# The last product of the first output tile, moved from VectorE to GpSimd in an encoder layer with a mixture of experts

## The chip, the cores and the metric

The kernel runs on one core of a Trainium2 chip. The metric is the device time of one execution in microseconds (us); three executions of the kernel before are given by their median. A profiled execution has a span of its own, from its first to its last instruction.

## What is computed

One layer of a bidirectional encoder on 512 tokens of width 1024, all in float32: attention in three dilated windows and a short gated convolution, a mixture of 32 experts of which each token takes 4, and a final RMS norm. What the change touches is the last line:

```python
def rmsnorm(x, g):
    xf = x.astype(jnp.float32)
    y = xf * lax.rsqrt(jnp.mean(xf * xf, axis=-1, keepdims=True) + RMS_EPS)
    return (y * g.astype(jnp.float32)).astype(g.dtype)
...
        x = x + merged @ w_out[l]
        x = x + moe_ffn(rmsnorm(x, ffn_norm_g[l]), w_router[l], b_router[l],
                        w_gate_up[l], b_gate_up[l], w_down[l], b_down[l])
    return rmsnorm(x, final_norm_g)
```

## The kernel before

The program is written out engine by engine, with semaphores by hand; each engine runs its instructions in the order written. It has a front (projections, attention, convolution, router), then a loop over the experts, and a tail that runs once.

**The loop.** For each expert, SyncE (SP) loads 12 MB of weights in pieces, TensorE (PE) multiplies up to 96 gathered tokens with them, VectorE (DVE) and ScalarE (ACT) apply bias, clamp and gate, and GpSimd (POOL) gathers the tokens of the next job by indirect DMA and adds the finished rows into `sum_rows` in DRAM (the scatter, L677). POOL also spreads the bias of the second product over the partitions with a broadcast (`spread_dn`, L684). `sum_rows` starts as the residual stream `x1`.

**The tail.** The last job's rows aren't scattered. Instead the four token tiles of `sum_rows` (t = 0 to 3, 128x1024 each) are loaded into `raw01` by SP (L542), once the scatter of the last job but one has landed (`y_stored`). PE multiplies the last job's result `y_last` with a matrix `last_pick` of gates, which places each row at its token, into the PSUM banks `fin_bank` (L1933). For the last tile it adds the loaded rows too, by two products with the identity (L1950).

DVE then makes, tile by tile, the final norm. For tile 0 to 2 it first adds `fin_bank` to the loaded rows (L1584 and L1586 for the halves of tile 0, `add_last`, L1580, for tiles 1 and 2). ACT squares the tile and sums (L997), DVE makes the variance (L1592), ACT its root (L1000), DVE the reciprocal (L1595), and DVE multiplies the tile by it and by the norm's weights `g_fin_row` in one operation, in place (L1600), or in two halves straight from `fin_bank` for tile 3 (L1605). The sum of tile t+1 stands in DVE's order ahead of the variance of tile t.

**Semaphores of the tail.** `sum_ready` counts the sums, `ss_f_ready` the sums of squares, `rstd_f_ready` the reciprocals, `out_ready` the finished outputs. SP's last loop waits for `out_ready` and stores one tile at a time (L545), then the two halves of the last (L549); the program ends when all five stores have landed. `ADDED` is 3. After its last broadcast POOL only waits for the scatter and the gathers.

```python
            for t in range(ADDED):
                sp.wait_ge(out_ready, t + 1)
                sp.dma_start(out[0, t * P:(t + 1) * P, :], raw01[:, t, 0:D_MODEL]).then_inc(out_stored, 16)
```

Of the kernel before, what the change touches and what calls it, by code (L numbers as in the profile page):

```python
# [30 lines left out]
ALU = mybir.AluOpType  # L31
# [3 lines left out]
SEQ, D_MODEL = 512, 1024  # L35
# [53 lines left out]
def build(nc, x, mix_norm_g, w_in, conv_w, attn_out_norm_g, conv_out_norm_g, w_out, ffn_norm_g,  # L89
# [14 lines left out]
    def sb(name, shape, dt=F32):  # L104
        return ctx.enter_context(nc.sbuf_tensor(name, shape, dt))

    def sem(name):
        return ctx.enter_context(nc.semaphore(name))
# [10 lines left out]
    with ctx:  # L119

        raw01 = sb("raw01", [P, RAW_FRONT, CHUNK])
# [21 lines left out]
        ss_f, std_f, rstd_f = (stats[:, 52 + TT * i:56 + TT * i] for i in range(3))  # L143
# [69 lines left out]
        g_fin_row = overlay(92 * K, ("g_fin_row", [P, D_MODEL], F32))  # L213
# [74 lines left out]
        g_fin_loaded = sem("g_fin_loaded")  # L288
# [3 lines left out]
        sum_ready = sem("sum_ready")  # L292
        sum_loaded = [sem(f"sum_loaded{t}") for t in range(TT)]
        ss_f_ready, var_f_ready, std_f_ready = sem("ss_f_ready"), sem("var_f_ready"), sem("std_f_ready")
        rstd_f_ready, out_ready, out_stored = sem("rstd_f_ready"), sem("out_ready"), sem("out_stored")


        def raw_slot(m):
# [50 lines left out]
        def fixed(eng, value):  # L349

            return value if isinstance(value, int) else eng.snap(eng.to_reg(value))
# [66 lines left out]
        PAIRS, ADDED = TT // 2, TT - 1  # L418
# [6 lines left out]
        def _(sp):  # L425
# [115 lines left out]
            for t in range(TT):  # L541
                sp.dma_start(raw01[:, t, 0:D_MODEL], sum_rows[t * P:(t + 1) * P, :]).then_inc(sum_loaded[t], 16)  # L542
            for t in range(ADDED):
                sp.wait_ge(out_ready, t + 1)
                sp.dma_start(out[0, t * P:(t + 1) * P, :], raw01[:, t, 0:D_MODEL]).then_inc(out_stored, 16)  # L545
            for n in range(2):
                cols = slice(n * 512, (n + 1) * 512)
                sp.wait_ge(out_ready, ADDED + n + 1)
                sp.dma_start(out[0, ADDED * P:TT * P, cols], raw01[:, ADDED, cols]).then_inc(out_stored, 16)  # L549
            sp.wait_ge(out_stored, 16 * (TT + 1))  # L550

# [2 lines left out]
        def _(pool):  # L554
# [128 lines left out]
            def spread_dn():  # L683
                pool.partition_broadcast(b_dn[:, 0:D_FF], b_dn[0:1, 0:D_FF]).then_inc(b_dn_spread, 1)  # L684
# [65 lines left out]
            pool.wait_ge(b_dn_loaded, dn_loads)  # L750
            gathered = fixed(pool, end * 16 * GROUPS)
            spread_dn()
            pool.wait_ge(y_stored, stored)
            pool.wait_ge(x_gathered, gathered)

# [248 lines left out]
        def _(dve):  # L1004
# [583 lines left out]
            for t in range(TT):  # L1588
                if t + 1 < ADDED:
                    add_last(t + 1)  # L1590
                dve.wait_ge(ss_f_ready, t + 1)
                dve.tensor_scalar(std_f[:, t:t + 1], ss_f[:, t:t + 1], 1.0 / D_MODEL, EPS, ALU.mult, ALU.add)\  # L1592
                   .then_inc(var_f_ready, 1)
                dve.wait_ge(std_f_ready, t + 1)
                dve.reciprocal(rstd_f[:, t:t + 1], std_f[:, t:t + 1]).then_inc(rstd_f_ready, 1)  # L1595
                dve.wait_ge(rstd_f_ready, t + 1)
                row = raw01[:, t, 0:D_MODEL]
                total = row if t < ADDED else fin_bank[:, 2 * t:2 * t + 2, :].rearrange("p two n -> p (two n)")
                if t < ADDED:
                    dve.scalar_tensor_tensor(row, total, rstd_f[:, t:t + 1], g_fin_row[:, :], ALU.mult, ALU.mult)\  # L1600
                       .then_inc(out_ready, 1)
                else:
                    for n in range(2):
                        cols = slice(n * 512, (n + 1) * 512)
                        dve.scalar_tensor_tensor(row[:, cols], total[:, cols], rstd_f[:, t:t + 1], g_fin_row[:, cols],  # L1605
                                                 ALU.mult, ALU.mult).then_inc(out_ready, 1)
# [371 lines left out]
```

## Time and profile before

| | us |
|---|---|
| median of 3 runs | 1280.15 (1278.89 to 1281.45) |
| the profiled execution, its own time | 1278.47 |
| its span | 1276.7 |
| TensorE busy in it | 1259.6 |
| VectorE busy | 582.8 |
| GpSimd busy | 316.6 |

The span lies within the execution's own time, which is 1.77 us longer. Rows of a timeline begin with the start of an instruction in us from the span's start and how long it took; a row that merges several (xN) has the time from the first's start to the last's end. In square brackets stands how long the engine was idle before, and what released it. An instruction's time includes a wait for a memory port, if it met one, but not its wait for semaphores. SPq is the queue on which SP issues transfers; the time in such a row is that of the issue.

### The profile page before, as it was taken

To read this page: it belongs to the slowest core of one execution; us is meant where nothing else is said; L and a number is where in the kernel's file an instruction comes from. 1 tells how busy PE (TensorE), PEld (TensorE's weight loads), DVE (VectorE), ACT (ScalarE), POOL (GpSimd) and SP (SyncE) were. 2 spreads that over 40 slices of the span, in tenths; PEclk is the share of its full clock that TensorE was granted. 3 is DMA by queue.
4 is the path that set the end of the run, shared out by engine and by line. 5 is a ranking of instruction groups with operands and counts; after the bars stand their busy time and mean duration, and the time that the engine had idled before them with its cause. 6 is when DMAs were issued, how large, how long until landed. Compare 5 with 4: busy or idle time off the path is not lost.

```text
span 1276.7 us, 32215 instructions
## 1 busy us (share of the span) xinstructions
PE 1259.6 (99%) x13814; PEld 666.2 (52%) x13814; DVE 582.8 (46%) x984; ACT 184.2 (14%) x279; POOL 316.6 (25%) x319
## 2 busy tenths in 40 slices
PE   8999999999999999999999999999999999999997
PEld 7867777844444444444444444444444433333343
DVE  7776666555433333333333333333344433333346
ACT  4243343410000000000000000000000000000002
POOL 2135533011333332222222222222222222222220
PEclk9999999999999999999999999999999999999999
DMA  9222117579999999999999999999999999999994
GB/s 261 78 65 65 67 68 283 232 295 410 409 420 416 411 421 421 416 422 417 415 421 418 417 419 423 421 422 421 426 421 421 421 419 420 422 421 417 422 382 160
DMA packets 73201, 450.30 MB, mean 353 GB/s; under 512 B 9744, under 2 KB 34816, under 8 KB 43472
## 3 DMA queue, kind: packets, MB, share of 16 engines
q1 hardware_dynamic: 62112, 430.46, 81.7%
q0 software_dynamic: 9568, 18.97, 5.6%
q10 hardware_dynamic: 1488, 0.40, 0.1%
q8 instruction: 24, 0.39, 0.1%
q14 instruction: 9, 0.07, 0.0%
HBM read 439.54 MB, written 18.67 MB: 359 GB/s over the span
## 4 chain that ended last, share of the span: by engine, by line
PE 82%; DMA 13%; DVE 3%; issue 1%; ACT 1%; POOL 0%; SPq 0%; DVEq 0%; POOLq 0%; ACTq 0%
PE gu_bank L1847 43%; PE bank L1862 20%; DMA raw<-in_w_gate_up_dram 12%; PE bank L1613 5%; PE bank L1615 4%; PE bank L1614 4%; PE bank L1697 1%; PE bank L1711 1%; PE bank L1674 1%; PE bank L1865 1%; DMA x_sb<-in_x_dram 1%; PE bank L1822 1%; DMA x_got<-xn_rows,gather_list 0%; PE first_gu_bank L1847 0%; DVE probs_a L1208 0%
## 5 line engine op out<-in xcount | busy, mean ns | idle before, releaser
L1847 PE MATMUL gu_bank<-raw,xT 128*32 128x512 f32 x2976 | 327.0, 592 | 2.7 <-DMA raw<-in_w_gate_up_dram 2.7
L1477 DVE TENSOR_TENSOR gate_in<-gu_bank,b_gu 128x768 f32<-128x768 f32 x31 | 29.7, 958 | 531.9 <-PE gu_bank L1847 531.9
L1847 PEld LDWEIGHTS gu_bank<-raw,xT 128*32 128x32 f32 x2976 | 111.4, 110 | 212.0 <-issue 198.1
L667 POOL DMA_INDIRECT x_got<-xn_rows,gather_list x96 | 114.4, 1192 | 291.8 <-DVE xT L1488 260.0
L1862 PE MATMUL bank<-raw_a,aT 128*32 128x256 f32 x2232 | 166.7, 379 | 0.0
L1862 PE MATMUL bank<-raw_b,aT 128*32 128x256 f32 x2232 | 166.7, 379 | 0.0
L1847 PE MATMUL gu_bank<-raw_c,xT 128*32 128x512 f32 x1488 | 166.0, 592 | 0.0
L1865 PE MATMUL bank<-raw_a,aT 128*32 128x256 f32 x744 | 165.6, 379 | 0.0
L1865 PE MATMUL bank<-raw_b,aT 128*32 128x256 f32 x744 | 165.6, 379 | 0.0
L1862 PEld LDWEIGHTS bank<-raw_a,aT 128*32 128x32 f32 x2232 | 107.1, 110 | 61.7 <-issue 16.3
L1862 PEld LDWEIGHTS bank<-raw_b,aT 128*32 128x32 f32 x2232 | 106.9, 110 | 48.7
L953 ACT ACTIVATE sig_in<-gate_in 128x768 f32<-128x768 f32 x32 | 27.1, 846 | 645.6 <-DVE gate_in L1481 645.6
L1847 PEld LDWEIGHTS gu_bank<-raw_c,xT 128*32 128x32 f32 x1488 | 56.3, 110 | 103.4 <-issue 101.5
L677 POOL DMA_INDIRECT sum_rows<-y_out,scatter_list x31 | 46.6, 1503 | 164.9 <-ACT y_out L961 108.9
L1847 PE MATMUL gu_bank<-raw_d,xT 128*32 128x512 f32 x744 | 86.2, 592 | 0.4 <-DVE xT L1494 0.4
L1847 PE MATMUL gu_bank<-raw_e,xT 128*32 128x512 f32 x744 | 86.2, 592 | 0.0
L961 ACT ACTIVATE y_out<-y_out,scatter_list 96x768 f32<-96x768 f32 (+1 forms) x62 | 44.8, 722 | 272.8 <-DVE y_out L1530 262.2
L1514 DVE STREAM_TRANSPOSE aT<-lin_in 128x192 f32<-128x192 f32 x128 | 60.6, 512 | 49.6 <-PE bank L1865 48.5
L1865 PEld LDWEIGHTS bank<-raw_b,aT 128*32 128x32 f32 x744 | 81.8, 110 | 0.0
L1865 PEld LDWEIGHTS bank<-raw_a,aT 128*32 128x32 f32 x744 | 81.8, 110 | 0.0
L1613 PE MATMUL bank<-xnT_hi,hi 128*128 128x512 f32 x160 | 66.5, 416 | 1.0 <-DVE xnT_lo L1135 1.0
L1615 PE MATMUL bank<-xnT_hi,lo 128*128 128x512 f32 x160 | 63.2, 395 | 0.0
(281 smaller groups left out, 1427.1 us busy)
## 6 DMA issues: line engine op xcount, KB each, us to landing
raw<-in_w_gate_up_dram SPq DMA_DIRECT2D x62, 2048.0 KB, 20.7
raw_a<-in_w_down_dram SPq DMA_DIRECT2D x31, 2048.0 KB, 21.6
raw_b<-in_w_down_dram SPq DMA_DIRECT2D x31, 2048.0 KB, 21.2
raw_c<-in_w_gate_up_dram SPq DMA_DIRECT2D x30, 2048.0 KB, 20.5
raw_d<-in_w_gate_up_dram SPq DMA_DIRECT2D x31, 1024.0 KB, 20.4
raw_e<-in_w_gate_up_dram SPq DMA_DIRECT2D x31, 1024.0 KB, 20.2
raw<-in_w_in_dram SPq DMA_DIRECT2D x24, 512.0 KB, 6.3
raw<-in_w_out_dram SPq DMA_DIRECT2D x8, 512.0 KB, 3.7
```

The source lines that it names most:

```text
L667: pool.indirect_dma_start(out=x_got[:, r, :], out_offset=None, in_=xn_quarters, in_offset=bass.IndirectOffsetOnAxis(ap=gather_list[:, r:r ...
L677: pool.indirect_dma_start(out=sum_rows, in_=y_out[0:TILE, :], in_offset=None, out_offset=bass.IndirectOffsetOnAxis(ap=scatter_list[0:TILE, ...
L953: act.activation(sig_in[:, :, :], gate_in[:, :, :], ACT.Sigmoid, scale=ALPHA).then_inc(sig_ready, 1)
L961: ins = act.activation(y_out[0:TILE, cols], y_out[0:TILE, cols], ACT.Copy, scale=scatter_list[0:TILE, 1:2].bitcast(F32))
L1477: dve.tensor_tensor(gate_in[:, :, :], gu[:, :, 0:QUARTER], gate_b, ALU.add)
L1514: dve.transpose(aT[:, 2 * i:2 * i + 2, :].rearrange("p k (r t) -> p k r t", r=GROUPS), lin_in[:, :, :].rearrange("p r (f k) -> p k r f", k ...
L1613: pe.matmul(dst, a_hi, b_hi, start=start, stop=False)
L1614: pe.matmul(dst, a_hi, b_lo, start=False, stop=False)
L1615: return pe.matmul(dst, a_lo, b_hi, start=False, stop=stop)
L1847: ins = pe.matmul(gu[c * GROUP:(c + 1) * GROUP, r, :], x[:, i, r * GROUP:(r + 1) * GROUP], w[:, c], start=first, stop=last)
L1862: pe.matmul(bank_[c * GROUP:(c + 1) * GROUP, cols], aT[:, k, c * GROUP:(c + 1) * GROUP], w[:, at:at + QUARTER], start=first and r % 2 == 0 ...
L1865: ins = pe.matmul(bank_[TILE:P, cols], aT[:, k, r * GROUP:(r + 1) * GROUP], w[:, at:at + QUARTER], start=first and r % 2 == 0, stop=last a ...
```

## The change

POOL takes over L1600 for t = 0, in two operations with a semaphore step between them: the tile times its reciprocal (one number for each partition), then the tile times the weights. It first waits for the weights' load, the sum, the sum of squares and the reciprocal of tile 0. DVE goes on to tile 1 right after the reciprocal. A new semaphore, `first_out_ready`, says that tile 0 is finished; SP waits for it before the first store, and for `out_ready` counts one lower before the others.

```diff
@@ sync: the stores
             for t in range(ADDED):
-                sp.wait_ge(out_ready, t + 1)
+                if t == 0:
+                    sp.wait_ge(first_out_ready, 1)
+                else:
+                    sp.wait_ge(out_ready, t)
                 sp.dma_start(out[0, t * P:(t + 1) * P, :], raw01[:, t, 0:D_MODEL]).then_inc(out_stored, 16)
             for n in range(2):
                 cols = slice(n * 512, (n + 1) * 512)
-                sp.wait_ge(out_ready, ADDED + n + 1)
+                sp.wait_ge(out_ready, ADDED + n)
@@ gpsimd: behind the last broadcast
             spread_dn()
+            pool.wait_ge(g_fin_loaded, 16)
+            pool.wait_ge(sum_ready, 1)
+            pool.wait_ge(ss_f_ready, 1)
+            pool.wait_ge(rstd_f_ready, 1)
+            made(pool.tensor_scalar(raw01[:, 0, 0:D_MODEL], raw01[:, 0, 0:D_MODEL], rstd_f[:, 0:1], None, ALU.mult))
+            pool.tensor_tensor(raw01[:, 0, 0:D_MODEL], raw01[:, 0, 0:D_MODEL], g_fin_row[:, :], ALU.mult)                .then_inc(first_out_ready, 1)
             pool.wait_ge(y_stored, stored)
             pool.wait_ge(x_gathered, gathered)
@@ vector: the final norm
                 dve.wait_ge(rstd_f_ready, t + 1)
+                if t == 0:
+                    continue
                 row = raw01[:, t, 0:D_MODEL]
```

GpSimd's built program, from its last copy to its end (the first word of a row is the line), before:

```order
L649 COPY last_list<-lists_sb 96x2
L351 ISA [waits b_dn_loaded]
L684 ISA b_dn<-b_dn 128x1024
L119 UNCONDITIONAL_BRANCH [waits x_gathered,y_stored]
```

and now (lines moved by 4):

```order
L653 COPY last_list<-lists_sb 96x2
L352 ISA [waits b_dn_loaded]
L688 ISA b_dn<-b_dn 128x1024
L761 ISA
L761 TENSOR_SCALAR raw<-raw,stats 128x1024 [waits ss_f_ready,rstd_f_ready,sum_ready,g_fin_loaded]
L762 TENSOR_TENSOR raw<-raw,g_fin_row 128x1024 [waits pool_step]
L119 UNCONDITIONAL_BRANCH [waits x_gathered,y_stored]
```

Beside the two operations one ISA instruction of L761 has come in, ahead of the waits; the diff doesn't name it.

VectorE's program from the sum of tile 1, now (`stats` holds the variances, roots and reciprocals; the lines are those of before plus 10 up to L1605, and plus 12 behind):

```order
L1590 TENSOR_TENSOR raw<-raw,fin_bank 128x1024 [waits fin_ready,sum_loaded1]
L1602 TENSOR_SCALAR stats<-stats 128x1 [waits ss_f_ready]
L1605 RECIPROCAL stats<-stats 128x1 [waits std_f_ready]
L1590 TENSOR_TENSOR raw<-raw,fin_bank 128x1024 [waits fin_ready,sum_loaded2,rstd_f_ready]
L1602 TENSOR_SCALAR stats<-stats 128x1 [waits ss_f_ready]
L1605 RECIPROCAL stats<-stats 128x1 [waits std_f_ready]
L1612 SCALAR_TENSOR_TENSOR raw<-raw,stats,g_fin_row 128x1024 [waits rstd_f_ready]
```

The product that stood between the first reciprocal and the sum of tile 2 is gone.

## Rows read from the trace of the kernel before

**Rows 1.** The page: span, and busy time of each engine.

```profile
span 1276.7 us, 32215 instructions
...
PE 1259.6 (99%) x13814; PEld 666.2 (52%) x13814; DVE 582.8 (46%) x984; ACT 184.2 (14%) x279; POOL 316.6 (25%) x319
```

**Rows 2.** Timeline of DVE in the tail: start, duration.

```profile
1264.51 1.22 DVE L1580 TENSOR_TENSOR raw<-raw,fin_bank 128x1024 f32<-128x1024 f32 x1 [0.24 <-PE fin_bank L1933]
...
1266.06 0.16 DVE L1595 RECIPROCAL stats<-stats 128x1 f32<-128x1 f32 x1 [0.27 <-ACT stats L1000]
1266.26 1.28 DVE L1600 SCALAR_TENSOR_TENSOR raw<-raw,stats,g_fin_row 128x1024 f32<-128x1024 f32 x1
1267.46 1.22 DVE L1580 TENSOR_TENSOR raw<-raw,fin_bank 128x1024 f32<-128x1024 f32 x1
...
1269.21 1.28 DVE L1600 SCALAR_TENSOR_TENSOR raw<-raw,stats,g_fin_row 128x1024 f32<-128x1024 f32 x1
...
1271.02 1.28 DVE L1600 SCALAR_TENSOR_TENSOR raw<-raw,stats,g_fin_row 128x1024 f32<-128x1024 f32 x1
...
1272.84 1.41 DVE L1605 SCALAR_TENSOR_TENSOR raw<-fin_bank,stats,g_fin_row 128x512 f32<-128x512 f32 x2
```

**Rows 3.** Timeline of SP's queue in the tail: when transfers are issued.

```profile
1258.77 1.75 SPq L542 DMA_DIRECT2D raw<-sum_rows  x4
1267.57 0.34 SPq L545 DMA_DIRECT2D out_dram<-raw  x1
...
1274.28 0.33 SPq L549 DMA_DIRECT2D out_dram<-raw  x1
```

**Rows 4.** From issue to landing: the stores of the output, then the loads of sum_rows.

```profile
DMA to landing us min/median/max: 2.0/2.6/2.6
...
DMA to landing us min/median/max: 3.5/4.9/5.9
```

**Rows 5.** Timeline of ACT: the sum of squares of tile 1.

```profile
1266.88 0.19 ACT L997 ACTIVATION_READ_ACCUMULATOR raw<-raw 128x1 f32 x1
```

**Rows 6.** Timeline of POOL: its last instruction.

```profile
1254.97 1.58 POOL L684 PARTITION_BROADCAST b_dn<-b_dn  x1
```

**Rows 7.** POOL's operations of the front, by line: duration ns min/median/max, first and last start.

```profile
L572 POOL TENSOR_SCALAR bias_h<-absd x6: 2454/2626/4585, 59.9 to 132.2; 128x896 f32<-128x896 f32 x6
...
L573 POOL TENSOR_TENSOR bias_h<-bias_h,log_m x6: 2128/2168/2517, 64.5 to 134.8; 128x896 f32<-128x896 f32 x6
...
L596 POOL TENSOR_SCALAR merged<-z_sb,conv_c x3: 1561/1567/2404, 111.7 to 186.7; 128x512 f32<-128x512 f32 x3
...
L599 POOL TENSOR_TENSOR merged<-merged,tap x6: 1272/1296/1307, 115.0 to 194.9; 128x512 f32<-128x512 f32 x6
```

**Rows 8.** Timeline of POOL: idle time before its first instruction, and before a first broadcast.

```profile
12.21 0.13 POOL L566 IOTA diff<- 128x1 int32 x1 [11.06 <-issue]
...
461.18 1.30 POOL L684 PARTITION_BROADCAST b_dn<-b_dn  x1 [6.23 <-issue]
```

**Rows 9.** Timelines of POOL and DVE where both work, in the front.

```profile
59.85 4.55 POOL L572 TENSOR_SCALAR bias_h<-absd 128x896 f32<-128x896 f32 x1 [38.60 <-DVE max_s L1194]
64.48 2.13 POOL L573 TENSOR_TENSOR bias_h<-bias_h,log_m 128x896 f32<-128x896 f32 x1
66.59 2.62 POOL L572 TENSOR_SCALAR bias_h<-absd 128x896 f32<-128x896 f32 x1
...
184.96 1.67 POOL L595 TENSOR_TENSOR z_sb<-gc_sb,u_sb 128x512 f32<-128x512 f32 x1 [21.62 <-DVE gc_sb L1151]
...
59.78 2.29 DVE L1121 TENSOR_TENSOR lo<-raw,hi 128x2048 fp32r<-128x2048 f32 x1
...
65.01 1.89 DVE L1208 TENSOR_SCALAR probs_a<-probs_a,rden 128x512 f32<-128x512 f32 x1
...
67.89 0.47 DVE L1208 TENSOR_SCALAR probs_a<-probs_a,rden 128x512 f32<-128x512 f32 x1
...
184.12 0.69 DVE L1151 COPY gc_sb<-bank 128x512 f32<-128x512 f32 x1 [1.56 <-PE bank L1615]
```

More of the change, by code:

```diff
@@ L295, in build @@
         rstd_f_ready, out_ready, out_stored = sem("rstd_f_ready"), sem("out_ready"), sem("out_stored")
+        first_out_ready = sem("first_out_ready")
         def raw_slot(m):
```

## The prediction

> **What bounds the kernel now.** I read first the span and the engines' busy shares [rows 1]: TensorE works for 99% of 1276.7 us, and weight streams feed it. The change touches none of that. It edits only what happens once, in the last eleven microseconds, so the reading goes to the end of the timeline, engine by engine.
>
> VectorE (DVE) there [rows 2] works through a chain: sum of a tile (L1580), variance, root on ScalarE, reciprocal (L1595), then the product with root and weights (L1600, 1.28 us for 128x1024). It is busy nearly without a gap from 1264.51 to 1274.25. Each tile's output is stored as soon as it is made [rows 3]: SyncE (SP) issues tile 0 at 1267.57, and the last half tile at 1274.28, 0.03 us after its last product (1272.84 + 1.41 = 1274.25). A 512 KB store lands 2.6 us after its issue, a 256 KB one 2.0 us after it [rows 4], so the last lands at 1276.28, and the span ends 0.4 us later. **The end is thus set by DVE's chain plus the last, smallest store; the three large stores before it are hidden because they leave early, spread over the chain.** GpSimd (POOL) has been idle since 1256.55 [rows 6].
>
> **What is removed.** One product of 1.28 us on DVE (L1600 for tile 0). Behind it stands the sum of tile 2, which started at 1267.46 [rows 2]; it can now start at 1266.26. ScalarE had the squares of tile 1 ready at 1267.07 (1266.88 + 0.19) [rows 5], so variance 1 comes right behind the sum, and each later DVE step comes 1.20 us earlier: the product of tile 1 at 1268.01 where it was at 1269.21. If nothing else held, DVE would end at 1273.05 and the span at 1275.5: a gain of 1.2 us. That is all that the removal can give.
>
> **What is added on POOL.** The reciprocal of tile 0 ends at 1266.22 [rows 2]. POOL starts 0.15 us after a DVE result (copy 184.12 + 0.69 = 184.81, POOL at 184.96) [rows 9], so at 1266.37. No row has a POOL operation of 1024 columns, so I extend two sizes [rows 7]: the multiply by a scalar takes 1.567 us for 512 columns and 2.454 us for 896 (its undisturbed minimum), 2.31 ns a column, giving 2.75 us for 1024. The tensor by tensor takes 1.296 and 2.168 us, 2.27 ns a column, giving 2.46 us. The step between them is 0.08 us (59.85 + 4.55 = 64.40 to 64.48) [rows 9]. Undisturbed, tile 0 is ready at 1266.37 + 2.75 + 0.08 + 2.46 = **1271.66**, against 1267.54 before.
>
> **POOL and DVE in each other's way.** The trace shows it [rows 9]. A POOL multiply at 59.85 takes 4.55 instead of 2.45 us while DVE runs an operation with two SBUF inputs until 62.07: it really begins at about 61.95. The other way round, a DVE multiply at 65.01 takes 1.89 instead of 0.47 us beside a POOL operation that ends at 66.61: it is let in about 0.2 us before that end. Here the product of tile 1 (two SBUF inputs: the row and the weights) arrives at 1268.01, inside POOL's first operation (to 1269.12). It is held to 1268.92, or gets in and delays POOL by about as much; it ends at 1270.20. POOL's second operation could start at 1269.20 but gets in only at 1270.08, and ends at **1272.54**. The bounds: nothing (1271.66) and, if DVE's next product got in as well, another 1.3 us. I take 1272.54, since in rows 9 whoever waits gets in as the holder finishes, and DVE waits first; its product of tile 2 comes only at 1268.92 + 1.81 (spacing of the products, 1269.21 to 1271.02) = 1270.73, when POOL runs.
> The Trainium skill (page SBUF — State Buffer, section Who interferes with whom) says that the shared ports are an exclusive lock for the whole instruction. The trace agrees for POOL's two-input operation, not for its multiply: a DVE multiply ran at 67.89 in its usual 0.47 us inside the POOL multiply of 66.59 to 69.21 [rows 9]. By that rule the product of tile 1 waits to 1269.12 instead of 1268.92, and the sum is +2.8 us.
>
> **What waits for tile 0.** SP issues the stores in order, and the wait for tile 0 now stands in front of all others. Tile 1, ready at 1270.20, and whatever follows wait behind it. So five stores of 2 MB leave together from 1272.57. The price of such a burst is in the loads of the four sum tiles, 2 MB issued together at 1258.77 to 1260.09 [rows 3]: the first lands after 3.5 us and the last 5.9 us after its own issue [rows 4] (the issues follow each other by 0.44 us), so three further tiles take 1265.99 − 1262.27 = 3.72 us. The first store lands after 2.6 us, the last then at 1272.57 + 2.6 + 3.72 = 1278.89, and the span ends 0.4 us later, at 1279.3. DVE's own end doesn't matter any more: its product of tile 2 is held by POOL's second operation until 1272.34, tile 3 follows 1.81 us behind at 1274.15 and is done at 1275.56; its last store alone would land at 1277.6.
> **Sum:** 1279.3 − 1276.7 = +2.6 us. The profiled execution took 1278.47 us, so 1281.1 by its measure. The median of the three runs shown is 1280.15; the forecast is 1280.15 + 2.6 = **1282.7**.
>
> **The extra instruction.** The built program has one more POOL instruction than the diff names, an ISA row between the broadcast and the multiply. Such a row stands also before the broadcasts and before L717. The first time that POOL goes from other work to the broadcast inside the loop, it is idle for 6.23 us with nothing in the trace to wait for; at the program's start 11.06 us [rows 8]. Here it comes before the waits, right behind the broadcast that ends at 1256.55, and so is over at 1262.8, or at 1267.6 if it takes 11.06. The first is hidden by 3.6 us of waiting for the reciprocal; the second is not. The Trainium skill (GPSIMD Engine Reference, Instruction dispatch) gives about 6 us for the load of a kernel's code that no profile instruction shows; the gap of 6.23 agrees.
>
> **Rivals.** (A) *No contention.* POOL and DVE pass each other; tile 0 is ready at 1271.66 and the sum is +1.7 us: 1281.9. For it: DVE's multiply that ran freely at 67.89. Against: an operation with two SBUF inputs, which delayed POOL by 2.1 us [rows 9]. (B) *POOL starts late or is slower:* the code load takes 11 us, or queues behind something that the rows don't show, so POOL begins at 1267.6, +1.2 us on the sum: +3.8 us, 1284.0. It decides if the load takes over 9.8 us. For it: 11.06 at the start. Against: 6.23 in the loop, with weight traffic beside it. (C) *Faster, by the shorter DVE chain:* −1.2 us, 1278.9. The place is SP's wait for tile 0; its point: the burst ends after tile 0 is ready by 0.03 + 2.6 + 3.72 + 0.4 = 6.75 us, so a gain of 1.2 needs tile 0 by 1268.8, both POOL operations in 2.4 us, and any gain at all needs it by 1269.95, in 3.6 us. Rows 7 say 5.2. That the change doesn't do what it says is excluded by the order of the built program.
>
> **How the numbers follow.** The main case has 0.60, A 0.20, B 0.15, C 0.05. A measurement of this kernel can tell about 0.2%, 2.56 us, from no change; the main case lies on that bound, and I give it 0.58 to be above (0.35), since the burst may have gaps. With B's 0.15 and 0.02 of A: slower 0.52, faster 0.05, within 0.2% 0.43. The range reaches from A less the 1.3 us by which the runs shown stray from their median (1280.15 + 1.7 − 1.3 = 1280.5) to B plus as much (1285.3).
>
> **What would show it.** After the change: the sum of tile 2 on DVE at about 1266.3; a POOL multiply at 1266.4 of 2.7 to 3.5 us and a POOL product ending near 1272.5, 3.3 to 3.4 us long as shown if its wait counts; the product of tile 1 on DVE of over 1.28 us, that of tile 2 held to over 2.5 us; five stores issued within about 3 us from 1272.6; an idle SP and idle DMA engines from 1268 to 1273. It is wrong if the stores of tiles 1 and 2 leave before tile 0, if POOL's first operation starts later than 1267, or if the last landing is set by DVE's last half.

## The result, and the profile after

The changed kernel takes 1284.43 us (median of 8 runs, 1282.91 to 1285.42), the kernel before beside it 1279.80 us (8 runs): a ratio of **1.0036, with a 95% interval of 1.0028 to 1.0045**. It is slower by 4.6 us where 2.6 were forecast. The profiled execution took 1283.37 us, its span is 1281.6 us at a granted clock of 0.997 of full speed (2.4 GHz), against 1276.7 us [rows 1]. So the span grew by 4.9 us.

The page after, span and busy time:

```profile
span 1281.6 us, 32220 instructions
...
PE 1264.7 (99%) x13814; PEld 875.1 (68%) x13814; DVE 586.4 (46%) x983; ACT 184.3 (14%) x279; POOL 322.0 (25%) x321
```

The busy times hardly help. POOL has its operations more, and DVE has lost an instruction and yet is busy for longer. PEld's 875 us against 666 [rows 1] catch the eye, but are not the change: the same changed kernel run again had 664.3, at the same ratio. The timeline tells where the time is.

DVE's timeline in the tail of the changed kernel (start, duration, engine, line, operation):

```profile
1262.79 0.69 DVE L1537 TENSOR_TENSOR y_last<-bank,b_dn 96x512 f32<-96x512 f32 x1 [3.06 <-PE bank L1877]
...
1267.40 1.22 DVE L1590 TENSOR_TENSOR raw<-raw,fin_bank 128x1024 f32<-128x1024 f32 x1 [0.24 <-PE fin_bank L1945]
...
1268.96 0.16 DVE L1605 RECIPROCAL stats<-stats 128x1 f32<-128x1 f32 x1 [0.27 <-ACT stats L1010]
1269.15 1.22 DVE L1590 TENSOR_TENSOR raw<-raw,fin_bank 128x1024 f32<-128x1024 f32 x1
...
1270.91 1.29 DVE L1612 SCALAR_TENSOR_TENSOR raw<-raw,stats,g_fin_row 128x1024 f32<-128x1024 f32 x1
...
1272.73 2.99 DVE L1612 SCALAR_TENSOR_TENSOR raw<-raw,stats,g_fin_row 128x1024 f32<-128x1024 f32 x1
...
1276.24 1.41 DVE L1617 SCALAR_TENSOR_TENSOR raw<-fin_bank,stats,g_fin_row 128x512 f32<-128x512 f32 x2
```

Its first row is the first sum of `y_last`, the bias added to the last expert's output. All that the change edits comes behind it. That row starts at 1262.79; before, it started at 1259.89:

```profile
1259.89 0.69 DVE L1527 TENSOR_TENSOR y_last<-bank,b_dn 96x512 f32<-96x512 f32 x1 [3.06 <-PE bank L1865]
```

**So 2.9 of the 4.9 us had been lost before the edited place was reached.** From that row to the end of the span it is 18.85 us, against 16.84 before: the other 2.0 us. I call this stretch the *tail* from here on, and give times in it from the start of that row.

The same two steps on POOL, and the stores on SP's queue (a row with x3 or x2 is that many issues in a row):

```profile
1269.34 2.86 POOL L761 TENSOR_SCALAR raw<-raw,stats 128x1024 f32<-128x1024 f32 x1 [9.89 <-DVE stats L1605]
1272.29 2.35 POOL L762 TENSOR_TENSOR raw<-raw,g_fin_row 128x1024 f32<-128x1024 f32 x1
```

```profile
1261.91 1.76 SPq L543 DMA_DIRECT2D raw<-sum_rows  x4
1274.66 1.65 SPq L549 DMA_DIRECT2D out_dram<-raw  x3
1277.02 1.77 SPq L553 DMA_DIRECT2D out_dram<-raw  x2
```

POOL ends at 1272.29 + 2.35 = 1274.64, 11.85 into the tail. The first store is issued 0.02 us later. Before, the first store left at 7.68 (1267.57 − 1259.89) and the last at 14.39 [rows 3]. Now nothing leaves until 11.87, then all five in 3.0 us (11.87, 12.26, 12.95, 14.23, 14.89), and from the first issue to the end of the span it takes 6.98 us. Only one finished tile stood behind tile 0: tile 1, made at 9.41. The product of tile 2 ended at 12.93 and the halves of tile 3 at 14.20 and 14.86, and each left within 0.03 us. So the last issue is just 0.5 us later than before; the other 1.5 us of the tail lie behind it, 3.96 us to the end of the span where they were 2.46. Their landings are later too, 3.6 us at the median where they were 2.6 [rows 4] (issue to landing, the stores of the output):

```profile
DMA to landing us min/median/max: 2.7/3.6/4.2
```

Where had the first 2.9 us gone? A landmark halfway is the first transposition `xT` of gathered rows, where the loop over experts begins. Before, and in the changed kernel:

```profile
282.57 1.61 DVE L1488 STREAM_TRANSPOSE xT<-x_got 128x768 f32<-128x768 f32 x1 [5.12 <-DMA x_got<-xn_rows,gather_list]
```

```profile
284.62 1.59 DVE L1498 STREAM_TRANSPOSE xT<-x_got 128x768 f32<-128x768 f32 x1 [5.00 <-DMA x_got<-xn_rows,gather_list]
```

It is 2.05 us late. I call the part before it the *front* (the expectations below call its end the first aT of the loop). (From there to `y_last`, through the loop over the experts, it takes 977.3 us before and 978.2 after. In the kernels below it lies between 977.5 and 979.1, so this is noise.) And the front's delay is there in the first 14 us. ScalarE there, before:

```profile
9.27 1.06 ACT L770 ACTIVATE sq_x<-x_sb 128x1024 f32<-128x1024 f32 x1 [1.51 <-DMA x_sb<-in_x_dram]
...
11.23 1.06 ACT L786 ACTIVATE hi<-raw 128x1024 fp32r<-128x1024 f32 x1 [0.21 <-DMA raw<-in_w_in_dram]
```

and after:

```profile
10.46 1.06 ACT L780 ACTIVATE sq_x<-x_sb 128x1024 f32<-128x1024 f32 x1 [2.66 <-DMA x_sb<-in_x_dram]
...
13.19 1.06 ACT L796 ACTIVATE hi<-raw 128x1024 fp32r<-128x1024 f32 x1 [0.98 <-DMA raw<-in_w_in_dram]
```

Both rows wait for a load, of the second half of x and of the first weights. The loads of x are issued at 0.8 and 1.3 us in both kernels, and what waits starts 1.19 and 1.96 us later than before. The diff touches nothing here. But POOL does something else. Before, it was idle for 11.06 us ahead of its first IOTA at 12.21 [rows 8], and issued the first of its nine loads of parameters at 12.66:

```profile
12.66 1.06 POOL L586 DMA_DIRECT2D g_merge<-in_attn_out_norm_g_dram  x1 [0.32 <-POOL diff L566]
```

In the changed kernel the idle time is gone and the same loads leave at 1.90 to 9.3 us:

```profile
1.44 0.14 POOL L570 IOTA diff<- 128x1 int32 x1 [0.29 <-issue]
1.90 1.06 POOL L590 DMA_DIRECT2D g_merge<-in_attn_out_norm_g_dram  x1 [0.32 <-POOL diff L570]
...
7.92 1.35 POOL L590 DMA_DIRECT2D w_r<-in_w_router_dram  x1
```

They share the DMA engines with what the chain waits for. The window from 0 to 12 us, before and after (the last two columns are the busy share of the DMA engines and GB/s):

```profile
0.00:12.00 12.00, 8.76 (x49) 8.36 (x50) 6.95 (x22) 4.96 (x9) 0.54 (x6) 1.00 0.87 266
```

```profile
0.00:12.00 12.00, 8.09 (x44) 7.69 (x44) 6.27 (x20) 3.99 (x7) 8.04 (x16) 1.00 0.89 216
```

The engines are as busy as before and move a fifth less. The parameters are scattered small pieces (`g_merge` is written as 128x4x1), which take time for few bytes: in this window POOL's queue has 7.4% of the DMA engines' time for 0.03 MB, and the other loads moved 2.56 MB where they moved 3.19.

The late load is not all of the 2.05 us. With the second half of x, PE transposes its tiles in 24 products. In the kernel before, in the changed kernel, and in the changed kernel run again:

```profile
11.49 2.84 PE L1631 MATMUL bank<-ident,x_sb 128*128 128x128 f32 x24 [1.53 <-DVE x_sb L1101]
```

```profile
12.68 4.49 PE L1643 MATMUL bank<-ident,x_sb 128*128 128x128 f32 x24 [2.68 <-DVE x_sb L1111]
```

```profile
12.72 5.27 PE L1643 MATMUL bank<-ident,x_sb 128*128 128x128 f32 x24 [2.87 <-DVE x_sb L1111]
```

They begin 1.19 us late, as x does, and then take longer, because PE's granted clock was halved, to 1.2 GHz, from 13.67 to 17.08 us (in the run again from 10.92 to 17.75). PE had stood idle for 2.68 us ahead of them, where it was 1.53. The clock stands in the third column from the end, for the window from 14 to 16 us before and after:

```profile
14.00:16.00 2.00, 0.96 (x7) 0.65 (x5) 1.63 (x4) 2.00 (x5) 2.00 (x4) 1.00 1.20 290
```

```profile
14.00:16.00 2.00, 2.00 (x11) 2.00 (x10) 1.38 (x2) 0.48 (x2) 0.00 (x0) 0.50 1.14 259
```

ScalarE's next step, `xnT_hi`, waits for PE's bank and starts at 15.77 where it was 13.66, 2.11 us late: 1.19 for the load of x and 0.92 for the clock. From there the delay stays within 0.1 us to the end of the front. The first weights, 1.96 us late, weren't what this step waited for. **A kernel edited in its last ten microseconds has got a different first seventeen.** The experiments had to show whether the change really does that, and through what.

### The profile page after: what moved, and what is told of

It is laid out like the page before. It is cut to its first block, busy times and chain, and to the rows that moved or that the text cites. A ratio compares the mean times of both kernels' runs of the same rounds, so it can differ in the third digit from the quotient of the medians.

```text
span 1281.6 us, 32220 instructions
## 1 busy us (share of the span) xinstructions
PE 1264.7 (99%) x13814; PEld 875.1 (68%) x13814; DVE 586.4 (46%) x983; ACT 184.3 (14%) x279; POOL 322.0 (25%) x321
## 4 chain that ended last, share of the span: by engine, by line
PE 94%; DVE 3%; DMA 1%; ACT 1%; issue 1%; POOL 0%; DVEq 0%; SPq 0%; POOLq 0%; ACTq 0%
PE gu_bank L1859 50%; PE bank L1874 22%; PE bank L1625 5%; PE bank L1627 4%; PE bank L1626 4%; PE bank L1877 4%; PE bank L1709 1%; PE bank L1723 1%; PE bank L1686 1%; DMA x_sb<-in_x_dram 1%; PE bank L1834 1%; DMA x_got<-xn_rows,gather_list 0%; PE first_gu_bank L1859 0%; DVE probs_a L1218 0%; DVE raw L1612 0%
## 5 line engine op out<-in xcount | busy, mean ns | idle before, releaser
L1859 PE MATMUL gu_bank<-raw,xT 128*32 128x512 f32 x2976 | 331.8, 592 | 0.0
L1859 PEld LDWEIGHTS gu_bank<-raw,xT 128*32 128x32 f32 x2976 | 200.1, 110 | 119.4 <-issue 21.9
L1874 PE MATMUL bank<-raw_b,aT 128*32 128x256 f32 x2232 | 173.9, 379 | 0.1
L1859 PE MATMUL gu_bank<-raw_c,xT 128*32 128x512 f32 x1488 | 172.2, 592 | 0.0
L1877 PE MATMUL bank<-raw_b,aT 128*32 128x256 f32 x744 | 169.8, 380 | 0.0
L1874 PEld LDWEIGHTS bank<-raw_a,aT 128*32 128x32 f32 x2232 | 124.3, 110 | 36.8 <-issue 1.0
L1874 PEld LDWEIGHTS bank<-raw_b,aT 128*32 128x32 f32 x2232 | 124.9, 110 | 34.1 <-issue 4.6
L1859 PEld LDWEIGHTS gu_bank<-raw_c,xT 128*32 128x32 f32 x1488 | 100.3, 110 | 59.6 <-issue 11.0
L1859 PE MATMUL gu_bank<-raw_d,xT 128*32 128x512 f32 x744 | 92.4, 593 | 0.3 <-DVE xT L1504 0.3
L1859 PE MATMUL gu_bank<-raw_e,xT 128*32 128x512 f32 x744 | 92.4, 592 | 0.0
L1877 PEld LDWEIGHTS bank<-raw_a,aT 128*32 128x32 f32 x744 | 81.8, 110 | 3.6 <-issue 0.4
L1877 PEld LDWEIGHTS bank<-raw_b,aT 128*32 128x32 f32 x744 | 79.9, 110 | 3.6 <-issue 0.8
L1859 PEld LDWEIGHTS gu_bank<-raw_e,xT 128*32 128x32 f32 x744 | 50.3, 110 | 29.8 <-issue 5.5
```

The costliest lines, as they stand in the source:

```text
L1859: ins = pe.matmul(gu[c * GROUP:(c + 1) * GROUP, r, :], x[:, i, r * GROUP:(r + 1) * GROUP], w[:, c], start=first, stop=last)
L1874: pe.matmul(bank_[c * GROUP:(c + 1) * GROUP, cols], aT[:, k, c * GROUP:(c + 1) * GROUP], w[:, at:at + QUARTER], start=first and r % 2 == 0 ...
L1877: ins = pe.matmul(bank_[TILE:P, cols], aT[:, k, r * GROUP:(r + 1) * GROUP], w[:, at:at + QUARTER], start=first and r % 2 == 0, stop=last a ...
```

## The experiments

Ten kernels in three sessions, each compared with the kernel before in its own session. The table gives, of the profiled execution, the start of `xT` (front), how long PE's granted clock was at 1.2 GHz in the front, the tail as defined above, and the ratio of the medians:

| kernel | POOL's first IOTA | front, us | at 1.2 GHz, us | tail, us | ratio (95%) |
|---|---|---|---|---|---|
| before | 12.21 | 282.57 | 0 | 16.84 | |
| changed | 1.44 | 284.62 | 3.4 | 18.85 | 1.0036 (1.0028 to 1.0045) |
| null_before | 11.71 | 282.12 | 0 | 16.85 | 1.0000 (0.9991 to 1.0009) |
| burst | 11.79 | 282.69 | 0 | 19.43 | 1.0027 (1.0015 to 1.0038) |
| beside | 1.44 | 285.64 | 6.8 | 18.31 | 1.0031 (1.0019 to 1.0043) |
| one_first | 1.44 | 285.37 | 3.4 | 18.15 | 1.0024 (1.0015 to 1.0033) |
| tiny | 1.45 | 284.48 | 3.4 | 16.84 | 1.0016 (1.0007 to 1.0025) |
| late_params | 1.44 | 281.90 | 0 | 18.86 | 1.0017 (1.0008 to 1.0026) |
| params_last | 11.91 | 282.43 | 0 | 16.86 | 1.0003 (0.9994 to 1.0012) |
| late_one_first | 1.44 | 282.24 | 0 | 17.55 | 1.0002 (0.9993 to 1.0011) |
| product_first | 1.44 | 282.93 | 0 | 16.34 | 0.9991 (0.9982 to 1.0000) |
| after_again | 1.44 | 285.48 | 6.8 | 18.84 | 1.0036 (1.0022 to 1.0050) |

### First session: the tail taken apart

**null_before** is the kernel before, unedited, for the noise.

> The kernel before, unchanged, for its spread and a second trace. The tail is counted from the start of the last result's first sum (y_last, 128x512 columns on DVE) to the end of the span: 16.8 us in the trace of before, 18.8 us after the change; ahead of it the changed kernel was 2.9 us later. Theory 1 (the 2.9 us are chance of an execution): this trace's y_last starts anywhere from 1259.9 to 1262.8 and PE's weight loads are busy anywhere from 666 to 875 us. Theory 2 (they belong to the built program, whose instructions lie elsewhere): y_last starts within 1 us of 1259.9, weight loads are busy near 666 us, ratio 1.000.

Measured: 1278.81 against 1278.95 us, a ratio of 1.0000 ± 0.0009. Front and tail repeat within 0.5 and 0.01 us. What follows: the tail can be read to some hundredths of a microsecond, the front to half a microsecond, the median to about one.

**burst** is the kernel before, with all work left on DVE; only the first store waits until three tiles are made.

```
-                sp.wait_ge(out_ready, t + 1)
+                sp.wait_ge(out_ready, max(t + 1, 3))
```

> The kernel before, but SP waits for three finished tiles before it issues the first store; nothing else moves and no work is added. Main theory (stores queued behind a late first one cost the tail): first store at 1272.3 of the old time scale, five stores together, last landing 6.3 to 6.6 us later, span end +2.6 us, ratio 1.0020, tail 19.4 us. Rival (DMA has room, the queue hides it): the last half tile's store alone sets the end, +0 us, tail 16.8. If the built program's place sets the loop, y_last may start elsewhere than in the kernel before, by up to 3 us.

SP's queue in burst:

```profile
1259.61 1.75 SPq L542 DMA_DIRECT2D raw<-sum_rows  x4
1272.92 1.65 SPq L545 DMA_DIRECT2D out_dram<-raw  x3
1274.61 2.44 SPq L549 DMA_DIRECT2D out_dram<-raw  x2
```

The burst starts at 1272.92 − 1260.48 = 12.44 of the tail and the span ends at 19.43, 6.99 us later. In the changed kernel that was 6.98. The tail of 19.43 meets the expectation. The ratio's interval, 1.9 to 4.9 us, holds the tail's 2.6; the front is that of before (282.69). (The medians differ by 4.1 us; the profiled execution was the fastest of its seven, and what the others have beyond 2.6 stays open.) What follows: late stores alone, with no POOL work at all, cost what they cost in the changed kernel. In both the end comes 7 us after *the first store leaves*, although DVE's last half is done 1.9 us behind that issue here and 3.0 us behind it there.

**beside** is the kernel before, which keeps its own product on DVE, and POOL does two operations of the same size into a free buffer. It writes results that nobody reads.

```
             spread_dn()
+            pool.wait_ge(g_fin_loaded, 16)
+            pool.wait_ge(sum_ready, 1)
+            pool.wait_ge(ss_f_ready, 1)
+            pool.wait_ge(rstd_f_ready, 1)
+            made(pool.tensor_scalar(raw_b[:, 0, 0:D_MODEL], g_fin_row[:, :], rstd_f[:, 0:1], None, ALU.mult))
+            made(pool.tensor_tensor(raw_b[:, 0, 0:D_MODEL], raw_b[:, 0, 0:D_MODEL], g_fin_row[:, :], ALU.mult))
```

> The kernel before with both POOL operations added beside the tail, at the same waits, on the weights' row and a buffer that is free, with a result nobody reads; DVE keeps all its products and SP waits for no POOL. Contention theory: POOL's first operation begins at the reciprocal of tile 0 together with DVE's product of tile 0, one of them is held by about 1.2 us, and a later DVE product is held by about 1.7 us behind POOL's second operation: tail 16.8 + 1 to 3 us. Rival (they pass each other): tail 16.8 to 17.2 us. If the code load behind the broadcast delays the scatter's landing, the load of the sum rows is issued 0.2 us later against y_last.

POOL and DVE in beside:

```profile
1269.89 3.83 POOL L757 TENSOR_SCALAR raw_b<-g_fin_row,stats 128x1024 f32<-128x1024 f32 x1 [9.89 <-DVE stats L1601]
1273.80 2.34 POOL L758 TENSOR_TENSOR raw_b<-raw_b,g_fin_row 128x1024 f32<-128x1024 f32 x1
```

```profile
1269.70 1.28 DVE L1606 SCALAR_TENSOR_TENSOR raw<-raw,stats,g_fin_row 128x1024 f32<-128x1024 f32 x1
...
1272.65 1.28 DVE L1606 SCALAR_TENSOR_TENSOR raw<-raw,stats,g_fin_row 128x1024 f32<-128x1024 f32 x1
...
1274.46 2.76 DVE L1606 SCALAR_TENSOR_TENSOR raw<-raw,stats,g_fin_row 128x1024 f32<-128x1024 f32 x1
```

Three pairings can be read. POOL's multiply started 0.19 us *after* a DVE product and took 3.83 us instead of 2.86: it was held for the 0.97 us more (by that product, not by the later one at 1272.65, since in the changed kernel a product inside the multiply cost it nothing). DVE's product at 1272.65 came when that multiply was already running, and passed in its usual 1.28. DVE's product at 1274.46 came during POOL's operation with two inputs, and took 2.76: it was held for 1.48. That last one lies on the path: 16.84 + 1.48 = 18.32, and the tail is 18.31. What follows: a DVE product holds up a POOL multiply that starts into it, and POOL's two-input operation holds up DVE's product. POOL's multiply, once running, neither held DVE nor was held.

**one_first** is the changed kernel with the stores in another order, so that tile 1 doesn't wait behind tile 0.

```
-            for t in range(ADDED):
+            for t in (1, 0, 2):
```

> The changed kernel, but SP stores tile 1 first, then tile 0, then the rest. Main theory (only the place in the store queue costs the tail its 2 us): stores leave at 1269.3, 1271.8, 1272.9 and so on of the old scale, the end is set by DVE's last half, which the hold of tile 2's product puts at 1274.8 instead of 1274.3: tail 17.3 us against 18.8 of the changed kernel, 1.5 us faster than it. Rival (the POOL operations and their contention cost it): tail stays 18.5 or more. The part ahead of the tail tells theory 2 from 1: within 0.5 us of the changed kernel's if program size sets it.

The tail fell from 18.85 to 18.15, less than expected. In this trace the whole tail had moved: the load of the summed rows was issued at +0.25, where before it was at −1.12 and after at −0.88, and the first reciprocal ends at 6.92 instead of 6.33, 0.6 us late. With that taken off it would be 17.6, and late_one_first below, where the load came at −0.90, has 17.55. What follows: about 1.3 of the tail's 2.0 us is the *order* of the stores, tile 1 behind tile 0; 0.7 remains. Of that, 0.5 is DVE, whose product of tile 2 is held for 1.7 us against the 1.2 gained, so that its last half is done at 14.87 instead of 14.36 (late_one_first); the other 0.2 lies behind the last issue.

### Second session: the front

In the table, POOL's first IOTA already splits the kernels in two. The front of those that begin at 1.44 was 284.6 to 285.6 in the first session, of the others 282.1 to 282.7; beside had it too, which shares with the changed kernel only POOL arithmetic near the end. Theory: that arithmetic belongs to other code than the broadcast before it. The built program has one more ISA instruction in front of it, so the code is changed at the end of the program. The next execution of the same program then finds the code for its IOTA in place, and doesn't wait. The trace of the kernel before bears on this. Its records of POOL's sequencer, which the views leave out, have a pair of instructions `MODIFY_POOL_CONFIG` 29 times: ahead of the first IOTA, of L717 and of 27 of the 32 broadcasts. POOL's next operation comes 11.1, 9.4, 7.0 and 5.9 us after the first four pairs, and 0.1 us after the other 25. At the first four the kind of work changes, from arithmetic to broadcast or back (at the IOTA, counted from the broadcast that ended the execution before); at the other 25 a broadcast follows a broadcast. In the changed kernel a thirtieth pair stands ahead of L761, and the first IOTA comes 0.1 us after the first pair. Rivals: the front's delay is chance, or comes from some other difference in the build.

The start of POOL's program is the same in both, an ISA instruction ahead of the IOTA included. Before:

```order
L565 MEMSET ident 128x128
L566 ISA
L566 IOTA diff 128x1
L586 DMA g_merge<-in_attn_out_norm_g_dram 128x4x1
```

In the changed kernel:

```order
L569 MEMSET ident 128x128
L570 ISA
L570 IOTA diff 128x1
L590 DMA g_merge<-in_attn_out_norm_g_dram 128x4x1
```

So the 10.8 us that differ there can't come from what stands in the program there.

**tiny** is the kernel before and one multiply of 128x1 as POOL's last instruction. Nobody waits for it, and it touches nothing that is read.

```
             spread_dn()
+            pool.tensor_scalar(sq_t[:, 0, 0:1], ones[:, 0:1], 1.0, None, ALU.mult)
```

> The kernel before with one POOL multiply of 128x1 on free memory behind the last broadcast, with no wait and nobody waiting for it. With it comes the same ISA row as in the changed kernel. Theory 3 (the code that POOL holds at the end of one execution is what it begins the next with): POOL's first IOTA at 1.4 us instead of 11.7 to 12.2, the nine parameter loads at 1.9 instead of 12.7, SP's first weight issues stretched (5th DMA at 6.0 to 6.3 instead of 5.1), the front 2 to 3 us longer (first aT of the loop at 284.5 to 285.6 instead of 282.1 to 282.7), tail 16.8 to 17.1 us, ratio 1.0015 to 1.0025. Theory 2 (program size or place) says a shift of any size with POOL's start as before. Theory 1 (chance): IOTA at 12, front as before, ratio 1.000.

POOL in tiny, at the start and at the end, and the landmark:

```profile
1.45 0.14 POOL L566 IOTA diff<- 128x1 int32 x1 [0.29 <-issue]
...
1257.76 1.58 POOL L684 PARTITION_BROADCAST b_dn<-b_dn  x1
1266.35 0.26 POOL L753 TENSOR_SCALAR sq_t<-ones 128x1 f32<-128x1 f32 x1 [7.01 <-issue]
```

```profile
284.48 1.62 DVE L1489 STREAM_TRANSPOSE xT<-x_got 128x768 f32<-128x768 f32 x1 [5.21 <-DMA x_got<-xn_rows,gather_list]
```

An instruction of 0.26 us at 1266, for which nobody waits, makes the kernel slower by 2.1 us (1281.84 against 1279.76). Its tail is to the hundredth that of before, and its front is 1.9 us later, with x 1.35 us late and 3.4 us of halved clock. The rivals fall. There is also the price of the change of code in its place: 7.01 us of idle time with nothing to wait for, over at 3.67 of the tail. The reciprocal comes at 6.3. So in the changed kernel it was hidden, as forecast.

The Trainium skill (GPSIMD Engine Reference, Instruction dispatch) puts the load of a kernel's code at about 6 us; 7.01 here agrees roughly, and 11.06 at the program's start [rows 8] doesn't.

**late_params** is the changed kernel, in which POOL's loads of parameters wait until x has been read, as they did by chance before.

```
+            pool.wait_ge(std_x_ready, 2)
             for dst, src in per_p:
```

> The changed kernel, but POOL's nine parameter loads wait until ACT has made both roots of the first norm (about 11 us), which is when they went out before the change. Theory 3 (early parameter loads collide with the loads of x and of the first weights): first IOTA still at 1.4, front back to 282.1 to 282.7, tail 18.8 unchanged, span 1278.5 to 1279, ratio 1.0015 against 1.0036 of the changed kernel. Rival (something else in the front is slower): front stays at 284.5 or later, ratio 1.0036.

POOL and ScalarE in late_params:

```profile
11.30 1.06 POOL L591 DMA_DIRECT2D g_merge<-in_attn_out_norm_g_dram  x1 [9.72 <-ACT stats L784]
```

```profile
8.86 1.06 ACT L781 ACTIVATE sq_x<-x_sb 128x1024 f32<-128x1024 f32 x1 [1.08 <-DMA x_sb<-in_x_dram]
```

With POOL just as early (IOTA at 1.44) but its loads at 11.30, the front is 281.90, that of before, and the window from 0 to 12 us moves 268 GB/s again. The tail stays at 18.86. The median is 2.3 us over before, a ratio of 1.0017. PE's clock is full there throughout the front, so the halved clock of the changed kernel came with the early loads too. So it is the early loads that cost, not the early POOL. And the two halves add up: tiny has +2.1 (front alone), late_params +2.3 (tail alone), together 4.4 of the changed kernel's 4.6.

**params_last** is the kernel before with its parameter loads issued even later, at 21 us, behind the first stage.

```
-            for dst, src in per_p:
-                pool.dma_start(dst, src, allow_slow_non_contiguous=True).then_inc(params_loaded, 16)
             pool.wait_ge(xnT_lo_ready, KD)
...
             pool.memset(z_sb[:, :], 0.0).then_inc(consts_made, 1)
+            for dst, src in per_p:
+                pool.dma_start(dst, src, allow_slow_non_contiguous=True).then_inc(params_loaded, 16)
```

> The kernel before with the nine parameter loads moved behind the normalized x (about 21 us instead of 12.7), no other change. If they also hold up the weight loads they meet from 12.7 us on, the front gets shorter by 0.2 to 1 us and the ratio is 0.9992 to 0.9999; if only x and the first weight chunk matter, ratio 1.000, front 282.1 to 282.7.

It came out as the second of the two cases: 1.0003 (0.9994 to 1.0012), and the front is 282.43, as before. At 12.7 us the loads were late enough already. There is nothing more to gain there.

**late_one_first** is the changed kernel with the edits of late_params and one_first together.

> The changed kernel with both remedies, tile 1 stored first and the parameter loads as in late_params. If both causes are right and add up: front 282.1 to 282.7, tail 17.5 us (18.15 if the scatter lands late again), ratio 1.0005 to 1.0010. If the front's 2 to 3 us don't come from the parameter loads: 1.0024 as one_first.

Front 282.24, tail 17.55, ratio 1.0002 (0.9993 to 1.0011). Both losses are mended but for 0.7 us of tail. The changed kernel's idea, two POOL operations, costs no measurable time when its two side effects are taken away, and gains none either.

### Third session: a version that uses POOL's idle time, and a repeat

**product_first** is late_one_first with POOL's operations exchanged and moved to the free buffer `raw_b`. The product with the weights needs only the sum, so it can run while the variance and the root are made; only the multiply by the reciprocal remains behind them. SP stores tile 0 from `raw_b`.

```
             pool.wait_ge(sum_ready, 1)
-            pool.wait_ge(ss_f_ready, 1)
+            made(pool.tensor_tensor(raw_b[:, 0, 0:D_MODEL], raw01[:, 0, 0:D_MODEL], g_fin_row[:, :], ALU.mult))
             pool.wait_ge(rstd_f_ready, 1)
-            made(pool.tensor_scalar(raw01[:, 0, 0:D_MODEL], raw01[:, 0, 0:D_MODEL], rstd_f[:, 0:1], None, ALU.mult))
-            pool.tensor_tensor(raw01[:, 0, 0:D_MODEL], raw01[:, 0, 0:D_MODEL], g_fin_row[:, :], ALU.mult)                .then_inc(first_out_ready, 1)
+            pool.tensor_scalar(raw_b[:, 0, 0:D_MODEL], raw_b[:, 0, 0:D_MODEL], rstd_f[:, 0:1], None, ALU.mult)\
+                .then_inc(first_out_ready, 1)
```

> The changed kernel with both remedies, and POOL multiplies tile 0 by the weights first, into a free buffer, as soon as the tile's sum stands (y_last + 4.4 us), and by the reciprocal afterwards. Its two-input operation then runs beside DVE work that reads PSUM, and its multiply beside DVE's product of tile 1, which passed it in the changed kernel. If the hold of DVE's product of tile 2 comes from POOL's two-input operation: that product takes 1.28 us instead of 2.98, tile 0 is ready at y_last + 9.5 to 9.9 instead of 11.8, DVE's last half is done at + 13.2 instead of 14.9, the tail is 15.7 to 16.3 us against 16.84 of the kernel before, ratio 0.9992 to 1.0000. Rival (any POOL operation holds DVE's two-input products): the product of tile 1 or 2 is still held by over 1 us, tail 17 us or more.

POOL, DVE's products and SP's queue in product_first:

```profile
1265.12 2.37 POOL L761 TENSOR_TENSOR raw_b<-raw,g_fin_row 128x1024 f32<-128x1024 f32 x1 [7.87 <-DVE raw L1598]
1267.60 2.86 POOL L763 TENSOR_SCALAR raw_b<-raw_b,stats 128x1024 f32<-128x1024 f32 x1
```

```profile
1268.71 1.29 DVE L1614 SCALAR_TENSOR_TENSOR raw<-raw,stats,g_fin_row 128x1024 f32<-128x1024 f32 x1
1270.53 1.28 DVE L1614 SCALAR_TENSOR_TENSOR raw<-raw,stats,g_fin_row 128x1024 f32<-128x1024 f32 x1
```

```profile
1270.02 0.34 SPq L550 DMA_DIRECT2D out_dram<-raw  x1
1270.48 0.35 SPq L550 DMA_DIRECT2D out_dram<-raw_b  x1
1271.84 0.33 SPq L550 DMA_DIRECT2D out_dram<-raw  x1
1273.12 1.05 SPq L554 DMA_DIRECT2D out_dram<-raw  x2
```

Tile 0 is ready at 1270.46 − 1260.59 = 9.87 of the tail (changed: 11.85), nobody is held (1.29 and 1.28), and the stores spread again from 9.43 on. The tail is 16.34, at the upper end of what was expected and 0.5 us *below* before, of the 1.2 that DVE's removed product could give. DVE's last half is done the full 1.2 us earlier (13.16 instead of 14.36), but the end of the span comes 3.15 us after the last issue, where it was 2.46: the stores are closer together, and the end is 6.9 us after the first issue, near the burst's 7.0. The ratio is 0.9991 (0.9982 to 1.0000): clearly faster than the changed kernel, and against the kernel before at the edge of what can be told.

**after_again** is the changed kernel, unedited, beside it.

> The changed kernel, unchanged, for a second trace and its time beside the others on one chip. If its cost is two pieces, front (parameter loads) and tail (stores behind the first), then the first aT of the loop is at 284.5 to 285.7, the tail 18.8 to 18.9 us (0.6 more if the scatter lands late), ratio 1.0033 to 1.0038. The loop between varies from 977.3 to 979.1 us in the traces so far whatever the kernel. Rival: the front's delay was chance, front 282 to 283, ratio 1.0015 to 1.0020.

1284.02 against 1278.74 us, 1.0036 (1.0022 to 1.0050), front 285.48, tail 18.84: the result and both its halves repeat.

## Why the prediction was right, and where it was not

The median lies inside the range, and the change is slower by more than 0.2%, the side that had the larger chance. But of 4.6 us the prediction accounts for 2. Step by step:

- **"What is removed": right.** The sum of tile 2 follows the reciprocal of tile 0 at once, 1269.15 behind 1268.96, and the first product of DVE starts 8.12 into the tail, where before it was the second at 9.32 [rows 2]: the 1.20 us. As forecast, it gave nothing in the changed kernel, where the burst of stores set the end.
- **"What is added on POOL": right in sum.** Forecast 2.75 and 2.46 us, measured 2.86 and 2.35; the longer and the shorter error cancel. The start was forecast 6.48 into the tail, and is 6.55.
- **"POOL and DVE in each other's way": the step that failed in the tail.** It said that the product of tile 1 is held by POOL's multiply and then holds up POOL's second operation, so that tile 0 is ready at 1272.54. Measured, on the same scale, is 1259.89 + 11.85 = 1271.74, and rival A without contention said 1271.66. DVE's product passed through POOL's multiply in 1.29 us. The rule read from [rows 9], whoever waits gets in as the holder finishes, was built from two pairs: a POOL multiply that came into a DVE operation, and a DVE multiply that came into POOL's *two-input* operation. A DVE product that comes into a POOL *multiply* is neither, and beside shows that it isn't held. The row that spoke for A, DVE's free multiply at 67.89, was the nearer one. The other half of the step was right: the product of tile 2 was held by POOL's two-input operation, to 2.99 us.
- The Trainium skill (SBUF — State Buffer, Who interferes with whom) has the exclusive lock on the ports that both share last for the whole instruction. The runs agree for POOL's two-input operation (DVE's product 2.99, 2.98 and 2.76 us instead of 1.28) and not for its multiply (1.29, 1.28 and 1.29 inside 2.86 and 3.83).
- **"What waits for tile 0": right in sum, not in the picture.** Five stores within 3 us, as forecast, but only tile 1 had been waiting; tiles 2 and 3 left as DVE made them. Forecast from the first issue to the end 2.6 + 3.72 + 0.4 = 6.7 us (6.75 from when tile 0 is ready), measured 6.98 and in burst 6.99. So the loads of the summed rows were a fair measure for a burst of stores, 0.25 us short.
- **The sum for the tail** is then: 2.6 forecast, 2.0 measured. Taken off, 0.8 for the contention that wasn't there; added, 0.25 for the burst.
- **"The extra instruction": right where it stands, wrong in what it does.** It was priced only in its place, where it is hidden (7.01 us, over well before the reciprocal). Rival B, that POOL starts late, is out. That the same instruction takes 11 us off the *start* of the next execution, and that this costs 2 us, was in no step and no rival. Nor was the halved clock, which is 0.9 of these 2 us in the profiled execution. The row that should have asked the question was quoted: 11.06 us of idle time before the first IOTA [rows 8]. It was used only as an upper bound for the price of a load of code.
- So the total has two errors of opposite sign: the contention priced at 0.9 and worth 0.1, and 2 to 2.7 us of front not seen. The median, 1284.43, lies nearer to rival B's 1284.0, which is out, than to the main case's 1282.7. That it lies inside the range is luck: B had widened the range for a reason that didn't occur.

What is shown and what is argued: that one POOL instruction at the end shifts POOL's start and costs 2 us is shown (tiny); that the cost runs through the early parameter loads is shown (late_params); its two parts, the late x and the halved clock, are read from the rows, and no run separates them; that the store order is the larger part of the tail's loss is shown by late_one_first. That POOL keeps something from one execution to the next is shown by the idle time that comes and goes with the last operation. That it is *loaded code* is inferred: the trace has the `MODIFY_POOL_CONFIG` instructions and the idle time behind them, but not what they do. Why the sum loads of one_first were issued 1.1 us later than elsewhere stays open.

## What to carry to other kernels

When a transfer is put behind a slower producer, look at who stands behind it in the same queue: here one ready tile did, and sending it first took back 1.3 of 2.0 us. Ask of every engine that became early what it will now start: 11 us of idle time that vanished at the program's start cost 2 us, since it had kept scattered parameter loads out of the way of the loads on the path, and such loads are better ordered by a wait than by luck. Read the granted clock there as well: a late load can cost more than its delay. And compare two traces from the front as well as around the edit; a landmark halfway and one just ahead of the edit, read in each kernel, splits the difference in a minute.

## What the runs showed of the hardware

- POOL's state at the end of an execution shows at the start of the next. With the broadcast as its last operation, the first IOTA comes at 11.7 to 12.2 us (four traces); with a multiply or product behind it, at 1.44 or 1.45 (eight traces of seven kernels, sizes 128x1 and 128x1024).
- Idle time for that change, in its place: 7.01 us in the tail (tiny), 6.23 in the loop [rows 8], 9.68 before the first broadcast at 298.37 us (kernel before). A broadcast that follows another broadcast has none of it (25 times 0.1 us).
- PE's granted clock fell to 1.2 GHz within the first 18 us in the five traces with early parameter loads, for 3.4 us in three and 6.8 us in two, and in none of the other seven. PE's idle time ahead of the 24 transpositions was 2.6 to 2.9 us in the five and 1.1 to 1.8 in the seven. The clock fell within it or up to 1.2 us behind it. The transpositions took 4.3 to 5.4 us instead of 2.8 to 2.9.
- The kernels with early parameter loads have a front of 284.5 to 285.6 us (five traces), the others 281.9 to 282.9 (seven traces): 2.7 us between the means, 285.1 and 282.4.
- At 128x1024, fp32, undisturbed: POOL's multiply by a scalar 2.86 us, its two-input product 2.35 to 2.37, DVE's product with root and weights 1.28. So a two-input operation on POOL is faster than a one-input one, and POOL needs about four times DVE's time for the same work in two steps.
- Who holds whom depends on the order of arrival and on POOL's operation: a POOL multiply that starts into a DVE product waits for it (+0.97 us), a DVE product that starts into a POOL multiply doesn't wait (+0.00), and one that starts into POOL's two-input operation waits (+1.48 to 1.71). A two-input operation of POOL that starts into a DVE product was in no run.
- Five stores of 2 MB in all take 7.0 us from the first issue to the end of the span, whether the first tile comes from DVE (burst) or from POOL (changed kernel, again, and in late_params): 6.97 to 6.99 in four traces.
